# The same transformer kernel with its activation tiles at multiples of 1024 bytes in on-chip memory

## What is computed

```
x = x + concat(rmsnorm(fox_attention(h)), rmsnorm(stick_breaking(h))) @ w_out   # h = rmsnorm(x) @ w_in
x = x + (silu(gate) * val) @ w_down        # gate, val = causal_dwconv(rmsnorm(x) @ w_up)
x = rmsnorm(x)
for i in range(2):                         # modulated by silu(c) @ w_ada[i] + b_ada[i]
    x = x + g_m * (moba_attention(h) if i == 0 else short_conv(h))
    x = x + g_f * swiglu(h2)               # FF width 2816
```

## The kernel before

| tile | first byte | its remainder by 1024 |
|---|---|---|
| `w_raw`, `w_hi`, `w_lo`, `res` | 16512, 49280, 65664, 82048 | 128 |
| `act_hi`, `act_lo`, `ada_raw`, `ada_acc`, `vec` | 90688, 98880, 107072, 123456, 148032 | 576 |
| all phase tiles (`scr`, `q_pad`, `hid_hi`, `q2`, ...) | 157504 and on | 832 (rows of `raw_hi`, `raw_lo`: 832, 64, 320, 576 in turn) |

## Time and profile before

### The profile page before, as it was taken

One profiled execution on the slowest core, in us unless ns is written; L12 is line 12 of the kernel. 1 busy time (PEld: TensorE's weight loads), 2 busy tenths in 40 slices (PEclk: granted clock), 3 DMA queues, 4 the chain that ended last, 5 costly groups with the idle time before them and its releaser, 6 DMA issues.

```text
span 909.7 us, 18262 instructions
## 1 busy us (share of the span) xinstructions
PE 900.3 (99%) x7367; PEld 875.8 (96%) x7367; DVE 749.3 (82%) x1032; ACT 503.3 (55%) x776; POOL 49.5 (5%) x87
## 2 busy tenths in 40 slices
PE   8999999999999999999999999999999999999998
PEld 7999999999999989999999999999999999999886
DVE  6999989999899789898987887987998887667544
ACT  6446757666665467764754444436645564444531
POOL 5100000000001000010000100100000000000000
PEclk9999999999999999999999999999999999999999
DMA  9887375666667947575469988984687467664541
GB/s 288 281 282 270 115 244 197 220 222 207 231 232 278 325 137 255 169 268 192 139 205 325 335 301 314 328 268 149 199 280 260 139 229 251 235 213 180 186 139 47
DMA packets 132129, 207.71 MB, mean 228 GB/s; under 512 B 4711, under 2 KB 109537, under 8 KB 126945
## 3 DMA queue, kind: packets, MB, share of 16 engines
q1 hardware_dynamic: 123968, 156.47, 51.3%
q0 software_dynamic: 8064, 50.34, 15.9%
q10 hardware_dynamic: 32, 0.01, 0.0%
HBM read 205.75 MB, written 1.05 MB: 227 GB/s over the span
## 4 chain that ended last, share of the span: by engine, by line
PE 91%; DVE 5%; ACT 2%; issue 1%; DMA 1%; SPq 0%; ACTq 0%; DVEq 0%
PE bank L1673 25%; PE bank L1675 25%; PE bank L1674 25%; PE bank L1828 2%; PE bank L1744 2%; PE bank L1753 2%; PE bank L1742 2%; PE bank L1710 1%; PE bank L1718 1%; PE bank L1712 1%; DVE w_lo L1002 1%; DMA w_raw<-in_w_in 1%; ACT w_hi L582 1%; PE bank L2028 0%; PE bank L2157 0%
## 5 line engine op out<-in xcount | busy, mean ns | idle before, releaser
L1002 DVE TENSOR_TENSOR w_lo<-w_raw,w_hi 128x1024 fp32r<-128x1024 f32 x294 | 353.8, 1221 | 107.6 <-ACT w_hi L582 105.4
L582 ACT ACTIVATE w_hi<-w_raw 128x1024 fp32r<-128x1024 f32 x293 | 306.1, 1056 | 242.3 <-PE bank L1675 226.7
L1673 PE MATMUL bank<-act_hi,w_hi 128*128 128x256 f32 x1312 | 366.1, 279 | 0.1
L1675 PE MATMUL bank<-act_hi,w_lo 128*128 128x256 f32 x1312 | 363.0, 277 | 0.0
L1674 PE MATMUL bank<-act_lo,w_hi 128*128 128x256 f32 x1312 | 363.0, 277 | 0.0
L1673 PEld LDWEIGHTS bank<-act_hi,w_hi 128*128 128x128 f32 x1312 | 246.5, 188 | 0.7 <-issue 0.6
L1674 PEld LDWEIGHTS bank<-act_lo,w_hi 128*128 128x128 f32 x1312 | 246.6, 188 | 0.4 <-issue 0.2
L1675 PEld LDWEIGHTS bank<-act_hi,w_lo 128*128 128x128 f32 x1312 | 246.6, 188 | 0.0
L1018 DVE SCALAR_TENSOR_TENSOR ada_acc<-ada_raw,silu_c,ada_acc 128x2048 f32<-128x2048 f32 (+1 forms) x56 | 114.3, 2040 | 1.7 <-DMA ada_raw<-in_w_ada 1.4
L1673 PE MATMUL bank<-hid_hi,w_hi 128*128 128x256 f32 x352 | 98.2, 279 | 0.0
L1674 PE MATMUL bank<-hid_lo,w_hi 128*128 128x256 f32 x352 | 97.2, 276 | 0.0
(11 more groups left out here) (309 smaller groups left out, 1374.0 us busy)
## 6 DMA issues: line engine op xcount, KB each, us to landing
w_raw<-in_w_gate_up SPq DMA_DIRECT2D x44, 1024.0 KB, 5.2
ada_raw<-in_w_ada POOLq DMA_DIRECT2D x40, 1024.0 KB, 5.3
w_raw<-in_w_down SPq DMA_DIRECT2D x33, 1024.0 KB, 5.1
w_raw<-in_w_in SPq DMA_DIRECT2D x23, 1024.0 KB, 6.8
w_raw<-in_w_up SPq DMA_DIRECT2D x22, 1024.0 KB, 5.7
w_raw<-in_w_qkv SPq DMA_DIRECT2D x12, 1024.0 KB, 7.3
w_raw<-in_w_out SPq DMA_DIRECT2D x8, 1024.0 KB, 7.0
ada_raw<-in_w_ada POOLq DMA_DIRECT2D x16, 512.0 KB, 4.9
```

The source lines that it names most:

```text
L582: act.activation(unit(w_hi, u), raw_half(c, h), ACT.Copy).then_inc(hi_ready, 1)
L1002: dve.tensor_tensor(unit(w_lo, u), raw_half(c, h), unit(w_hi, u).bitcast(F32), ALU.subtract).then_inc(lo_ready, 1)
L1673: pe.matmul(dst, a_hi, b_hi, start=start, stop=False, skip_group_check=True)
L1675: return pe.matmul(dst, a_lo, b_hi, start=False, stop=stop, skip_group_check=True)
```

## The change

No instruction is added, removed, or put in another place; the instruction streams of all engines are the same. Only addresses differ. Four small tiles (`gain2`, `rowsum`, `nmax`, `q_rstd`: 128 + 128 + 128 + 64 = 448 bytes) are declared ahead of `act_hi`, so it moves up by 448 bytes. `fold`, `stack`, `rinv` and `nlf` go to the top of memory, above the largest phase, by way of a place holder of 70 rows that is given back at once; the phases then begin 832 bytes lower.

```
         silu_c = sb("silu_c", [P, KT])
         silu_e = sb("silu_e", [P, KT])
+        gain2 = sb("gain2", [P, 4, KT])
+        rowsum = sb("rowsum", [P, 16, 2])
+        nmax = sb("nmax", [P, 16, 2])
+        q_rstd = sb("q_rstd", [P, 4, 4])
         act_hi = sb("act_hi", [P, KT, T], F32R)
         act_lo = sb("act_lo", [P, KT, T], F32R)
...
-        gain2 = sb("gain2", [P, 4, KT])
         qk_gain = sb("qk_gain", [P, 1])
         q_rms = sb("q_rms", [P, 3, 4])
-        q_rstd = sb("q_rstd", [P, 4, 4])
...
-        rowsum = sb("rowsum", [P, 16, 2])
-        nmax = sb("nmax", [P, 16, 2])
-        rinv = sb("rinv", [P, 16, 2])
...
-        nlf = sb("nlf", [P, 2, 8])
         f_cum = sb("f_cum", [P, 2, 8])
-        fold = sb("fold", [P, P])
-        stack = sb("stack", [P, 32])
+        phase = ExitStack()
+        phase.enter_context(nc.sbuf_tensor("below_top", [P, 70 * T], F32))
+        fold = sb("fold", [P, P], stack=phase)
+        stack = sb("stack", [P, 32], stack=phase)
+        rinv = sb("rinv", [P, 16, 2], stack=phase)
+        nlf = sb("nlf", [P, 2, 8], stack=phase)
+        phase.close()
```

## The result

The changed kernel takes 940.0 us (median of four runs, 939.5 to 941.6) against 913.3 us of the kernel before (four runs, 910.9 to 913.9). The ratio is 1.030, with a 95% interval of 1.029 to 1.032. The forecast was 913.4 us and "no change"; the range of 901 to 925 us does not hold the result.

A forecast was written before the change was run, and what follows sets the result against it. TensorE's matmul stream was taken as the bound: number of matmuls times the distance between their starts. All terms summed to 0, leaving a span of 909.7 us and a median of 913.4 us; range 901 to 925 us.

The forecast's parts named there:

- What bounds the kernel: Whole span: TensorE busy 99%, hardly waiting; time is number of matmuls times pitch, the distance between starts of two matmuls.
- splits, DMAs and waits: Splits L582 and L1002 touch only tiles that stay; DMA bytes and number unchanged, TensorE's DMA waits 0.9 us: 0 us.
- The step that failed: Moving rows of act, hid, ot, fox, raw1 going to remainder 0: 5832 matmuls, pitch taken as unchanged, 0 us.
- the rival "slower": Moving row and standing slice read at once, relative placement counts: 27 us, 940 us (chance 0.06), or 916 to 922 (0.14).
- the far bound of 27 us: Largest loss for the moved row starts: 118 - 113.3 = 4.6 ns on each of 5832 matmuls.
- The slow pitch of attention, 118: Second model's attention: same instructions at 117.6 to 119.4 ns between starts instead of 113.3, put down to how the stream started.
- The value chunks and the last layer: 384 value-chunk matmuls and 264 of 512 columns: the weights move and stay, a standing slice's start costs nothing, 0 us.
- The weight load as pacer: TensorE's matmul stream: loading 128 fp32 columns takes about 112 ns whatever moves, so a stall-free stream saves about 1 ns per matmul.
- the bounds on a gain: Moved row starts: at most 1.3 ns per matmul, down to the weight load's pace, x 5832 = 7.6 us.
- The 258 columns: 288 matmuls moving raw rows at 120.5 ns: one crossing before and now, crossings not the cost; 0 us, at most 2.1 either way.

## Why the prediction was wrong

**What bounds the kernel** held: the time is the number of matmuls times the pitch, and the whole difference is in the pitch. Nothing else moved: splits, DMAs and waits cost 0, as put.

**The step that failed** is the value taken for the moved row starts: "I take 0: three row starts (576, 832 and 128) give one and the same pitch". The three are no sample of all starts, and the third was one fast chunk: of the fifteen runs of value matmuls in that trace two are at 113.4 ns, the others at 117.7 to 121.5. Taken as distances to the slice that is loaded beside them they are 192, 192 and, for the value chunks, 64 modulo 256, the only two distances of the table at which 113.3 ns occurs. The sentence that would have shown this stood in the text, in the rival "slower": both distances are "64 more than a multiple of 128; now by a whole multiple of 128. No row shows that case." A case that no row shows had been given the value of the rows that are there. In the place of 0 the step measured 27.4 us over 5856 matmuls, 4.7 ns each, on the far bound of 27 us that had been worked out for it.

**The rival "slower"** was right in what counts, how moving row and standing slice lie to each other, and in its sum: 940 us, 940.0 measured. That it is the weight loads which are held is not shown: a load lasts 188 ns on average in both traces. Its size was right partly by chance. The slow pitch of attention, 118, was taken for all. In truth the fast streams go from 113.3 to 118.6 (761 matmuls in 165 to 255 us and not the 766 named for it), and those that had been slow already lose little: one of 78 matmuls at 127 us goes from 118.7 to 119.7 ns. What spoke against it, that fast and slow pitch occur at one distance, was true and did not bear on it: the distance gives the set of pitches, and something else picks one of them. A chance of 0.06 for it was too low.

**The value chunks and the last layer** were also put at 0, because a standing slice may start anywhere. That holds for the slice alone, as the even pitch over slices at 128 and 640 shows (these are 512 apart, two periods). But there too the distance changed: 0.4 and 0.9 us.

**The weight load as pacer.** That a load paces TensorE at "about 112 ns whatever moves" was read from one group of rows, and the same trace has a faster one, eight fp32 transposes of 128 columns with a weight load for each:

```profile
124.96 1.03 PE L2103 MATMUL bank<-ident,o_tok 128*128 128x128 f32 x8
```

One of them lasts 0.27 us, so seven distances take 0.76 us, 109 ns each. So 112 ns is no floor under every load, and the bounds on a gain that were worked out from it, 7.6 us and "not 6.7", had no firm ground. What did hold is that no distance tried gave 256 columns less than 113.3 ns (the 113.0 above is that within its 0.5 ns). The gap of N / 2.4 + 2.5 ns, which the Trainium skill has for a warm matmul (TensorE: Matmul & The Clock Gate, Back-to-back issue gap), 109.2 ns here, was not reached at any of the eight distances. The section gives it for a matmul by itself and says that in a stream of weight loads and matmuls both set the spacing, so this stream does not test it.

**The 258 columns** told, rightly, that crossings of 1024 bytes are not the price: before and after, each such row crosses one, and its 288 matmuls got 0.3 us slower in all nevertheless.

**Known and open.** That the distance sets which pitches there are is shown. Why those, and what picks one where there are two, is not.

## What to carry to other kernels

In a stream of fp32r matmuls with 256 moving columns, a new weight load for each one, the placement of the tiles sets the pace: only where the start of the moving row was 64 or 192 bytes modulo 256 above that of the slice which is loaded meanwhile did the fast pitch occur. It did not occur everywhere there: at 64 one kernel lost 19 us, at 192 one lost 12 us. And with 512 moving columns other distances are good. So such a placement has to be measured, not only computed. When a tile is added or removed ahead of such operands, compare these differences before and after; a shift of the activations by 64 bytes cost 3.8% here with not one instruction changed. And when an operation is priced by rows that all agree, ask what they have in common before giving their value to a case that none of them shows.

## What the runs showed of the hardware that was not expected

- The pace of a matmul stream depends on the distance between the start of the moving operand and that of the weights loaded meanwhile. Shown by the pair with identical activation addresses: weights' halves at 192 modulo 1024, 113.4 ns; at 128, 120.1 ns. The likely reason is that TensorE's own two reads hold each other up; no trace records the reads, so this is inferred. The Trainium skill says that TensorE and ScalarE never wait on anyone (SBUF — State Buffer, Who interferes with whom). Against other engines the traces agree, with 118.6 and 118.7 ns whether VectorE and ScalarE stand or work. The Trainium skill also says of TensorE's two read ports that loading the next weights takes no read bandwidth from the running matmul (TensorE: Matmul & The Clock Gate, Step-by-step: what each phase is for). With this the pair above does not agree, if the inference holds.
- The effect repeats after 256 bytes (`act_*` at 0 and at 768 of 1024: 934.46 and 934.61 us, both at 118.6 and 120.0 ns) and is not monotonic: 113.4, 120.1, 118.6 ns at 64, 96 and 128.
- At five of the eight distances (32, 64, 128, 160, 192) a stream has two stable pitches. Apart from the two kernels with two distances in one stream, every stream of 300 and more matmuls settles within about two dozen and keeps its pitch, the longest over 960 matmuls. What picks it, and what in the memory has a period of 256 bytes, stays open.
- No arrangement tried beats the kernel before; lifted as a whole by 64 bytes it runs the same (910.65 and 910.71 us).
